# Dilated attention of a two-block transformer kernel: the probabilities are scaled in rows before they are turned

## What is computed

```python
for g, (window, dil) in enumerate(DILATED_PAIRS):
    o, m, d = band_attention(qb[:, g], kb[:, g], vb[:, g], dil, window)
...
wgt = d * jnp.exp(m - m.max(axis=0, keepdims=True))
wgt = wgt / wgt.sum(axis=0, keepdims=True)
return jnp.einsum('gsh,gshd->shd', wgt, o)
```

## Time and profile before

| what | value |
|---|---|
| median of 3 runs | 1077.38 us (1077.21 to 1077.56) |
| the profiled execution, its own time | 1077.18 us |
| span of the profiled execution | 1075.2 us |
| TensorE busy | 1065.3 us (99%) |
| VectorE busy | 805.4 us (75%) |
| ScalarE busy | 664.1 us (62%) |
| GpSimd busy | 85.0 us (8%) |

### The profile page before, as it was taken

The page is one execution under the profiler, slowest core; times in us unless marked ns, Lnnn a source line. Parts: engine busy times, 40 slices in busy tenths (PEclk is TensorE's granted clock), DMA queues, the critical chain, the costliest instruction groups (busy, mean ns, idle before and its releaser), DMA issues.

```text
span 1075.2 us, 18058 instructions
## 1 busy us (share of the span) xinstructions
PE 1065.3 (99%) x6332; PEld 898.2 (84%) x6332; DVE 805.4 (75%) x1418; ACT 664.1 (62%) x1160; POOL 85.0 (8%) x103
## 2 busy tenths in 40 slices
PE   9999999999999999999999999999999999999998
PEld 8977888888878888888889988888877789888887
DVE  5987775665667768666766888888876757988886
ACT  6477654445466567566566666666666756666664
POOL 0000000000000000100010021221001000221220
PEclk9999999999999999999999999999999999999999
DMA  9642566666646563455515666566553435656562
GB/s 320 192 137 83 173 209 188 190 191 182 193 118 216 160 209 103 136 178 176 183 54 160 188 202 193 172 200 195 155 180 118 138 119 175 212 180 195 179 194 96
DMA packets 117774, 183.88 MB, mean 171 GB/s; under 512 B 6864, under 2 KB 70736, under 8 KB 117584
## 3 DMA queue, kind: packets, MB, share of 16 engines
q1 hardware_dynamic: 117280, 182.77, 54.3%
q10 hardware_dynamic: 432, 0.29, 0.1%
HBM read 181.99 MB, written 1.05 MB: 170 GB/s over the span
## 4 chain that ended last, share of the span: by engine, by line
PE 90%; DVE 6%; ACT 4%; issue 1%; POOL 0%; ACTq 0%; DVEq 0%; POOLq 0%
PE ps L781 17%; PE ps L730 11%; PE ps L731 10%; PE ps L733 10%; PE ps L786 9%; PE ps L845 5%; PE ps L847 5%; PE ps L846 5%; DVE w_lo L2062 2%; PE ps L1068 1%; PE ps L924 1%; DVE hid L2640 1%; PE ps L999 1%; ACT w_hi L1388 1%; PE ps L784 1%; PE ps L785 1%
## 5 line engine op out<-in xcount | busy, mean ns | idle before, releaser
L2062 DVE TENSOR_TENSOR w_lo<-w_stage,w_hi 128x1024 fp32r<-128x1024 f32 x336 | 414.3, 1249 | 137.2 <-ACT w_hi L1388 136.4
L1388 ACT ACTIVATE w_hi<-w_stage 128x1024 fp32r<-128x1024 f32 x336 | 351.5, 1056 | 159.7 <-PE ps L733 75.6
L786 PE MATMUL ps<-aT,w_lo 128*128 128x256 f32 x990 | 278.4, 281 | 0.0
L781 PE MATMUL ps<-aT,w_hi 128*128 128x512 f32 x766 | 271.3, 398 | 0.0
L730 PE MATMUL ps<-w_hi,aT 128*128 128x512 f32 x480 | 192.4, 401 | 1.5 <-DVE aT L2076 1.3
L786 PEld LDWEIGHTS ps<-aT,w_lo 128*128 128x128 f32 x990 | 187.6, 189 | 0.9
L731 PE MATMUL ps<-w_lo,aT 128*128 128x512 f32 x480 | 187.0, 390 | 0.0
L733 PE MATMUL ps<-w_hi,aT 128*128 128x512 f32 x464 | 181.1, 390 | 0.0
L781 PEld LDWEIGHTS ps<-aT,w_hi 128*128 128x128 f32 x766 | 143.9, 188 | 35.4 <-issue 0.2
L730 PEld LDWEIGHTS ps<-w_hi,aT 128*128 128x128 f32 x480 | 90.1, 188 | 23.7 <-issue 5.0
L845 PE MATMUL ps<-w_hi,u_hi 128*128 128x512 f32 x272 | 106.6, 392 | 0.0
(11 more groups left out here) (281 smaller groups left out, 1295.6 us busy)
## 6 DMA issues: line engine op xcount, KB each, us to landing
w_stage<-in_ffn_w_up SPq DMA_DIRECT2D x88, 512.0 KB, 4.5
w_stage<-in_a_w_qkv SPq DMA_DIRECT2D x72, 512.0 KB, 4.0
w_stage<-in_ffn_w_down SPq DMA_DIRECT2D x44, 512.0 KB, 3.6
w_stage<-in_w_up SPq DMA_DIRECT2D x32, 512.0 KB, 3.6
w_stage<-in_w_down SPq DMA_DIRECT2D x32, 512.0 KB, 3.5
w_stage<-in_b_w_qkv SPq DMA_DIRECT2D x24, 512.0 KB, 4.1
w_stage<-in_w_in SPq DMA_DIRECT2D x23, 512.0 KB, 5.0
w_stage<-in_w_out SPq DMA_DIRECT2D x8, 512.0 KB, 3.6
```

Of the source, the lines that this page charges most:

```text
L781: pe.matmul(ps[:, bank(stg, names[f]), :], wh, aT[:, k, :, :].rearrange("p a s -> p (a s)"), start=(k == 0), stop=False)
L786: last = pe.matmul(o, wl, aT_hi[:, k, :], start=False, stop=(k == KT - 1))
L1388: act.activation(w_hi[:, slot, :], w_in[:, slot, :], ACT.Copy).then_inc(hi_done[slot], 1)
L2062: dve.tensor_tensor(w_lo[:, slot, :], w_in[:, slot, :], w_hi[:, slot, :].bitcast(F32), ALU.subtract).then_inc(lo_done[slot], 1)
```

## The change

`ATTENTION_COUNTS` and the lists of all four engines change; only `half_a0` and `half_a1` use them. The reciprocals are now taken per unit (two sums). GpSimd multiplies the exponentials of a unit's head 0 in place by the reciprocals of their rows (`scale_left`), VectorE those of head 1 (`scale_right`); both read and write `score_ring` in SBUF, 128x384 elements. A transpose of head 0 now waits for the semaphore `left`, one of head 1 for `right`, where both waited for `prob`. GpSimd's broadcast, the two transposes of the sums per pair, ScalarE's copy of them, and VectorE's product of the outputs are gone. ScalarE copies the high part straight from bank 7 (`summed_hi`), and VectorE subtracts the low part for all pairs and then frees bank 7 (`summed_lo`); GpSimd's `low_part` is no longer used in this stage.

```diff
--- before.py
+++ after.py
@@ -244,7 +244,7 @@
 
 
 JOINED_COUNTS = {"prob": 8, "rd": 4, "rdb": 4, "bc": 4, "ohi": 4, "olo": 4}
-ATTENTION_COUNTS = {"prob": 16, "rd": 4, "rdb": 4, "bc": 4, "ohi": 4, "olo": 4}
+ATTENTION_COUNTS = {"prob": 16, "rd": 8, "left": 8, "right": 8, "ohi": 4, "olo": 4}
 
 
 def make_plan():
@@ -453,7 +453,7 @@
             "rows_late", "gate_in", "first_in", "first_hi", "first_lo", "stored", "ln_norm", "ln_post", "hiT", "mh", "ms", "rstd", "rtok", "conv", "act_step", "dve_step",
             "gates", "lnf", "rot", "cv", "ecv", "mqk", "prob", "peak", "pd", "oms", "wm",
             "orstd", "osq", "hms", "dm", "ovar", "sig", "sq", "ms8", "rs8", "silu", "u", "uhi", "ulo", "msq", "pms", "prstd", "x_new",
-            "half", "scaled", "r2", "lam", "zeroed", "const_ready", "gate_w", "unit", "rd", "rdb", "bc", "ohi", "olo")}
+            "half", "scaled", "r2", "lam", "zeroed", "const_ready", "gate_w", "unit", "rd", "rdb", "left", "right", "bc", "ohi", "olo")}
 
 
         def is_full(stg, name, i=0):
@@ -995,19 +995,12 @@
                     if n % 4 == 0:
                         pe.wait_ge(*is_free(stg, f"p{n // 4}{j}"))
                     if t == 0:
-                        pe.wait_ge(s["prob"], at(stg, "prob", 4 * j + 2 * i + h + 1))
+                        done = ("left", "right")[h]
+                        pe.wait_ge(s[done], at(stg, done, 2 * j + i + 1))
                     last = pe.transpose(ps[:, b, n % 4 * P:(n % 4 + 1) * P],
                                         score_ring[units[2 * j + i]["ring"]][:, h, t * P:(t + 1) * P], ident)
                     if n % 4 == 3:
                         last.then_inc(full[b], 1)
-
-            def turn_pair_sums(stg, j):
-
-                b = bank(stg, f"o{j}")
-                pe.wait_ge(s["rdb"], at(stg, "rdb", j + 1))
-                for qt in range(TOK):
-                    last = pe.transpose(ps[:, b, S + qt * P:S + (qt + 1) * P], rden_wide[:, j % 3, qt * P:(qt + 1) * P], ident)
-                return last
 
             def pair_values(stg, units, j):
 
@@ -1045,12 +1038,10 @@
                         between([0])
                     if k:
                         pe.wait_ge(*is_free(stg, f"o{k - 1}"))
-                        pair_values(stg, units, k - 1)
-                        turn_pair_sums(stg, k - 1).then_inc(full[bank(stg, f"o{k - 1}")], 1)
+                        pair_values(stg, units, k - 1).then_inc(full[bank(stg, f"o{k - 1}")], 1)
                     turn_pair(stg, units, k)
                 between(range(1, KT // 2))
                 pe.wait_ge(*is_free(stg, f"o{n - 1}"))
-                turn_pair_sums(stg, n - 1)
                 pair_values(stg, units, n - 1).then_inc(full[bank(stg, f"o{n - 1}")], 1)
 
             def heads_ready(halves):
@@ -1497,6 +1488,13 @@
 
             def attention_pairs(stg, units, last):
 
+                def summed_hi(k):
+
+                    un = units[2 * k]
+                    act.wait_ge(*is_full(stg, f"o{k}"))
+                    act.activation(heads_to(oT_hi, un), heads_from(ps[:, bank(stg, f"o{k}"), 0:S], un), ACT.Copy)\
+                        .then_inc(s["ohi"], 1)
+
                 def first_turned(k):
 
                     b = bank(stg, f"p0{k}")
@@ -1510,15 +1508,13 @@
                 for k in range(1, n):
                     if k + 1 < n:
                         exps(stg, units[2 * k + 2], 2 * k + 2)
-                    keep_sums(stg, k - 1)
                     if k + 1 < n:
                         exps(stg, units[2 * k + 3], 2 * k + 3)
                     else:
                         split(stg, last)
                     first_turned(k)
-                    heads_hi(stg, units[2 * k - 2], k - 1)
-                keep_sums(stg, n - 1)
-                heads_hi(stg, units[2 * n - 2], n - 1)
+                    summed_hi(k - 1)
+                summed_hi(n - 1)
 
             def evac_v(stg, name, i, dst, scale, src=None):
                 act.wait_ge(*is_full(stg, name, i))
@@ -2014,14 +2010,13 @@
                 for j in range(n - 3, n - 1):
                     low_part(stg, units[j], j)
 
-            def wide_pairs(stg, units):
-
-                n = len(units) // 2
-                for k in range(n):
-                    wide_part(stg, k)
-                    if k >= 2:
-                        low_part(stg, units[2 * k - 4], k - 2)
-                low_part(stg, units[2 * n - 4], n - 2)
+            def scale_left(stg, units):
+
+                for u, un in enumerate(units):
+                    pool.wait_ge(s["rd"], at(stg, "rd", u + 1))
+                    sc, c = score_ring[un["ring"]][:, 0, 0:3 * P], 2 * (u % 2)
+                    pool.tensor_tensor(sc, sc, stat(f"rden{u // 2 % 3}", 4)[:, c:c + 1].broadcast_to([P, 3 * P]), ALU.mult)\
+                        .then_inc(s["left"], 1)
 
             A4, B4 = [f"a{f}" for f in range(4)], [f"b{f}" for f in range(4)]
 
@@ -2041,7 +2036,7 @@
                     scale_up(S_, i, B4, 2)
 
             for hf in range(2):
-                wide_pairs(st[f"half_a{hf}"], list(units_a(hf)))
+                scale_left(st[f"half_a{hf}"], list(units_a(hf)))
             scale_ffn("a")
             for hf in range(2):
                 wide_parts(st[f"half_b{hf}"], list(units_b(hf)))
@@ -2196,23 +2191,51 @@
                         heads_scaled(stg, u - 2)
                 last_low(stg, units[n - 1], n - 1)
 
+            def scale_right(stg, un, u):
+
+                c = 2 * (u % 2)
+                rd = stat(f"rden{u // 2 % 3}", 4)
+                if u >= 6:
+                    dve.wait_ge(s["left"], at(stg, "left", u - 5))
+                dve.wait_ge(s["prob"], at(stg, "prob", 2 * u + 2))
+                dve.reciprocal(rd[:, c:c + 2], stat(f"den{u // 2 % 2}", 4)[:, c:c + 2]).then_inc(s["rd"], 1)
+                dve.wait_ge(s["rd"], at(stg, "rd", u + 1))
+                sc = score_ring[un["ring"]][:, 1, 0:3 * P]
+                dve.tensor_scalar(sc, sc, rd[:, c + 1:c + 2], None, ALU.mult).then_inc(s["right"], 1)
+
+            def summed_lo(stg, un, j):
+
+                b = bank(stg, f"o{j}")
+                dve.wait_ge(s["ohi"], at(stg, "ohi", j + 1))
+                dve.tensor_tensor(heads_to(oT_lo, un), heads_from(ps[:, b, 0:S], un), heads_to(oT_hi, un).bitcast(F32),
+                                  ALU.subtract).then_inc(s["olo"], 1)
+                dve.wait_ge(s["olo"], at(stg, "olo", j + 1))
+                dve.sem_inc(drained[b], 1)
+
             def attention_pairs(stg, units, last):
 
                 n = len(units) // 2
                 for k in range(n):
+                    if k == 0:
+                        scale_right(stg, units[0], 0)
+                        scale_right(stg, units[1], 1)
                     if k + 1 < n:
                         for u in (2 * k + 2, 2 * k + 3):
                             maxima(stg, units[u], u)
-                    reciprocals(stg, k, 4 * k + 4, k % 2)
-                    if k:
-                        heads_scaled(stg, k - 1)
+                        if k:
+                            scale_right(stg, units[2 * k + 2], 2 * k + 2)
                     for m in (1, 2):
                         b = bank(stg, f"p{m}{k}")
                         dve.wait_ge(*is_full(stg, f"p{m}{k}"))
                         dve.tensor_copy(prob[:, m, :], ps[:, b, :]).then_inc(drained[b], 1)
+                    if k + 1 < n:
+                        if k == 0:
+                            scale_right(stg, units[2], 2)
+                        scale_right(stg, units[2 * k + 3], 2 * k + 3)
+                    if k:
+                        summed_lo(stg, units[2 * k - 2], k - 1)
                 split(stg, last)
-                heads_scaled(stg, n - 1)
-                last_low(stg, units[2 * n - 2], n - 1)
+                summed_lo(stg, units[2 * n - 2], n - 1)
 
             def sum_square(un, v):
```

## The result

The changed kernel takes 1093.47 us (median of 4 runs, 1093.09 to 1094.15), the kernel before 1077.30 beside it (1077.20 to 1077.56): a ratio of 1.0148, interval 1.0136 to 1.016. It is slower by 16.2 us. The forecast was 1084.4 us with a range up to 1092.0: the sign was right, and the time lies 1.5 us outside the range.

The account below looks back on a forecast made before the run. TensorE was taken as the bound. Its removed transposes save 1.1 us a half, but late scalings and bank 7's release make each half 3.6 us longer net; 2 x 3.6 = 7.2 us on 1077.18 gives 1084.4 us, range 1079.2 to 1092.

Parts of the forecast that it names:

- What bounds the kernel: In the changed stage TensorE is busy 23.00 of 23.00 and 25.00 of 25.00 us, so every wait is lost in full.
- VectorE's then goes first, since it sits right behind the reciprocal: At the two scalings one reciprocal releases, VectorE runs before GpSimd; they exclude each other; a half is 3.6 us longer.
- the second rival: GpSimd goes first each time; VectorE's eight scalings a half each wait 1.0 us; 9.6 us a half, 1096.4 us; chance 10%.
- The durations: Added work: GpSimd's scaling 1.01 us, VectorE's 0.41, a reciprocal 0.17, the subtraction of the low part 0.63.
- steps 1 and 2: Stretches of each half: values of pair 1 go at 429.5 against 426.06, of pair 2 at 434.7 against 430.61.
- What goes: TensorE loses two transposes of sums per pair, 0.28 to 0.30 us each pair: 1.1 us a half, 2.3 us in all.
- The start: At the start of a half the first transposes go 0.9 us late, the second six 1.6 us late, behind the scalings.
- The wait for bank 7: Values of pairs 1 and 2 wait 1.7 and 0.8 us for VectorE's subtraction, which frees the bank.
- The maxima: On VectorE in step 0 they start at 419.55, not 417.99, behind the scaling; those of step 2 queue behind the subtraction.
- The clock: Rival without its own chance or price: new waits, up to 1.7 us each, lower the clock; inside the range's upper end.
- What would show it: Signs in the trace: TensorE's waits for scalings and subtraction, idle time up 9.5 us, work down 2.3; VectorE's scaling times.
- the third: Sign of the second rival, counted among all cases: VectorE's scalings all take 1.4 us; chance 10%.

Follow-up runs that it names:

- experiment 1: Changed kernel with GpSimd's scaling of head 0 waiting for VectorE's scaling of the same unit instead of the reciprocal: 1083.93 us.
- Experiment 5: Changed kernel with VectorE scaling units 0 and 1 inside the projection, before its last two instructions there: 1090.88 us.
- experiment 6: Changed kernel with VectorE's subtraction, which frees bank 7, moved ahead of its scaling of the odd unit: 1090.17 us.
- experiment 7: Changed kernel with idle TensorE products, 16 in step 2 and 5 in step 3, ahead of the values: 1092.63 us.
- experiment 8: Kernel before the change, with each pair's two transposes of sums issued twice: 1079.29 us, ratio 1.0018.
- experiment 11: Changed kernel with GpSimd's scaling behind VectorE's, ScalarE freeing bank 7, and units 0 and 1 scaled inside the projection: 1077.42 us.
- experiment 4: Changed kernel with VectorE scaling both heads of each unit and GpSimd none: 1087.38 us.
- experiments 9 and 10: On experiment 4, ScalarE frees bank 7 and GpSimd subtracts three pairs' low parts: 1083.25 us; then units 0 and 1 also scaled inside the projection: 1081.36 us.

## Why the prediction was wrong, step by step

**What bounds the kernel** was right: TensorE had no idle time in the stage, and whatever it waits for is lost.

**The step that failed** is one sentence: "VectorE's then goes first, since it sits right behind the reciprocal." That the two scalings exclude each other for a whole instruction was right, and so was the consequence if VectorE goes first: experiment 1 makes it so, has the forecast waits at the forecast places, and gives 1083.9 us for the 1084.4 forecast. But GpSimd had the shared way in 16 of 16 pairs (and in all of experiments 5, 6 and 7). VectorE then stands 0.67 us in each of its eight scalings of a half instead of in two. An estimate from experiment 1 says what that makes. There VectorE stands in two scalings of a half, 0.59 us each. In the changed kernel six stand ahead of the first release of bank 7 and eight ahead of the second, 0.67 us each: 2.8 and 4.2 us more. Experiment 1 has the values of pairs 1 and 2 late by 2.9 and 3.5 us, so they should be late by 5.7 and 7.7 us, and a half longer by 3.1 + 4.2 = 7.3; the trace has 5.7, 8.1, and 7.6 and 7.9 for the two halves. GpSimd first was the second rival, with a chance of 10%; its argument against, that GpSimd "has to be woken by another engine's semaphore", was true (0.04 us, 418.70 against 418.66) and did not decide. The rival's 1096.4 was too long because it took 1.0 us for each stand, where 0.67 was measured.

The Trainium skill, page "SBUF — State Buffer", section "Who interferes with whom", says that in this pair the instruction issued first keeps the shared ports for its whole length and the other fully blocks. The trace agrees with the blocking (1.09 us against 0.42 alone). With "first" it does not, if the start of a row is taken for the issue: VectorE's rows start 0.04 us earlier, and VectorE is the one that stands. When an instruction really asks for the ports isn't in the trace.

How near the two must be for that is on record, with VectorE's subtraction for the low part of a weight in the place of its scaling. The kernel before has both orders in its feed-forward stage. In the earlier trace rows VectorE's row starts at 700.79 and that of GpSimd's second product at 700.78 (the end of the two, less 0.74 us), and VectorE stands (1.80 us). A little later VectorE is 0.14 us ahead (706.83 against 706.97, the end of GpSimd's row less the 1.72 us of its second product), takes its own 1.26 us, and GpSimd stands:

```profile
706.27 2.42 POOL L2033 TENSOR_TENSOR o_sb<-xn,o_sb 128x256 f32<-128x256 f32 x2 [4.76 <-DVE xn L2510]
```

```profile
706.83 1.26 DVE L2062 TENSOR_TENSOR w_lo<-w_stage,w_hi 128x1024 fp32r<-128x1024 f32 x1 [0.39 <-ACT w_hi L1388]
```

All fourteen traces agree: where VectorE's subtraction or scaling meets a GpSimd product or subtraction, VectorE takes its own time if its row starts 0.126 us or more ahead of GpSimd's, and stands if it starts within 0.045 us ahead of it or shortly behind; no pair lies between. The scalings, 0.04 us ahead, are on the losing side of that gap. So "goes first" was worth 0.04 us of lead, and that was too little.

**The durations.** GpSimd's scaling: 1.01 taken, 0.83 measured (inside the ends of 0.735 and 1.29). VectorE's: 0.41 taken, 0.42 measured. The reciprocal of two sums: 0.17 taken, 0.15 to 0.17 measured. The subtraction: 0.63 taken, 0.57 measured in steps 1 and 2, but with 0.33 us behind it in step 1 in which VectorE waits for its own semaphore (its next row is at 432.78), which the forecast left out. None of them is the error.

**What goes** was too high: 1.1 us a half, from differences of starts. Adding the same work costs 0.22 to 0.23 us a pair (experiment 8). Taking it away saves as much, where no wait stands in between: in experiment 11 the values of pairs 1, 2 and 3 go at 427.75, 432.09 and 439.14, so they are 4.34 and 7.05 us apart, before 4.55 and 7.51; that is 0.21 for one pair of transposes and 0.46 for two. TensorE's busy time fell by 0.72 us a half and not by four times 0.22; that its pieces no longer overlap at the two waits would explain the rest, but wasn't tested. In the timeline of before the six transposes behind the sums start 0.65 us ahead of the next six (423.17 and 423.82); in experiment 11, with no sums ahead of them, this distance is 0.69 to 0.71. So part of the price of changing from the values to transposes had been put down to the sums; whoever is first behind the values pays it.

**The start** was right in kind: 0.5 and 0.9 us late for 0.9 and 1.6 forecast, less because GpSimd is faster and never waits. Experiment 5 takes it away and wins 2.6 us, some of it by an earlier start of the stage itself.

**The wait for bank 7** was right in its place and cause, 3.1 and 0.9 us for 1.7 and 0.8. Its excess is VectorE's standing: six scalings lie ahead of the first release, of which the forecast let two stand. Four more, at 0.67 us each, are 2.7 us, and the release is 5.7 - 3.4 = 2.3 us later than forecast.

**The maxima** were forecast to be late with nobody waiting for them on TensorE's side. In fact the scores of units 4 and 6 wait 0.39 and 0.32 us a half for VectorE (L2152) to free their bank. This step was left out.

**The clock** was named as a rival without a price and put inside the upper end. It did fall to 1.2 GHz behind the wait of 3.1 us, in both halves: the window 434 to 436 stands at 0.50, that from 436 to 438 at 0.67, the next at 1.00. Its price was 1.2 us in a half of experiment 4 and 1.6 in one of experiment 6, where TensorE has the next piece to itself; in the changed kernel, where VectorE is the bound, about 0.25 us are seen in the first half (experiment 7), and 0.3 and 0.6 us a half are left over by the estimate above. So it isn't what makes the result 9 us longer than the forecast. Whether it carried the result over the edge of the range is open: the estimate without it is 1077.2 + 2 x 7.3 = 1091.8 us, and the stage began 0.8 us late. The range was too short at its upper end: its own text had 1096.4 as a case of one in ten and ended at 1092.0.

**"What would show it"** worked: "VectorE's scalings ... all at 1.4 us (the third)" is what the trace has, at 1.09 us. The forecast that TensorE's idle time would grow by 9.5 us was near (some 12 us), but it missed that TensorE's busy time would grow as well (by 1.8 us in the first half).

What stays open: why 0.04 us ahead is not enough, and how much earlier VectorE's scaling itself must start. With VectorE's subtraction 0.13 us was enough. A scaling was ahead by that much only where GpSimd had been made to wait for its end, and in experiments 9 and 10, where one that started 0.26 us ahead of GpSimd's subtraction took its own 0.42 us; nothing between 0.045 and 0.26 us was seen for it.

## What to carry to other kernels

When one event releases work on VectorE and on GpSimd that both need the shared way to SBUF, don't count on an order: make GpSimd wait for VectorE's instruction if VectorE is the busier engine. Here that wait was worth 9.5 us of 1093. Then look at what else GpSimd does beside VectorE: in experiments 9 and 10 its subtraction made VectorE stand again. Work that is moved ahead of its reader may be small and on idle engines, and still be dear, if the engine that does it also frees a bank that the bound engine needs; and in a sum, an engine that was busy 63% of the stage (14.46 of 22.79 us) can become the bound of two steps when each of its instructions stands for a partner.

What an added or removed instruction on TensorE is worth is the change in the distance between the pieces around it, not the distance of two starts: 0.21 to 0.23 us here, read as 0.28.

## What the runs showed of the hardware beyond that

- VectorE's scaling of 128x384 by a scalar per row, from SBUF to SBUF, takes 0.42 us alone and 1.08 to 1.09 us when a GpSimd scaling of 0.83 us is released with it: it starts its own work about 0.2 us before the end of GpSimd's row (418.66 + 1.08 - 0.42 = 419.32, against 418.70 + 0.83 = 419.53).
- A wait of 2.51 us before the same work was followed by the lower clock in one half and by the full clock in the other, within one execution (experiment 4); so was one of 1.94 us (experiment 6). So the length of a wait alone does not say what follows.
